# Loads at the start of a fused transformer kernel: parameter columns first, input rows in four parts, a shorter run of filler products, and the sum of the first norm later in the first weight unit

## The reference, cut to what matters

```
def rmsnorm(x, g):
    y = x * rsqrt(mean(x * x, axis=-1) + EPS)
    return y * g

h = rmsnorm(x, ab_norm)
z = h @ w_in                       # 1024 -> u, gate, q, k, v (512 each) and 8 forget logits
u, gate, q, k, v, f_logit = split(z)
y_a = rg_lru(causal_depthwise_conv(u, conv_w, conv_b), ...) * gelu(gate)
```

## Time and profile before

| | |
|---|---|
| median of three runs | 1609.82 us (1608.34 to 1611.64) |
| profiled execution, its own time | 1608.58 us |
| its span on the core | 1606.8 us |
| TensorE matmuls busy | 1447.0 us (90%) |
| VectorE busy | 765.9 us (48%) |
| ScalarE busy | 297.5 us (19%) |
| mean traffic | 247 GB/s |

### The profile page before, as it was taken

How to read it: one execution, slowest core, us unless ns; L and a number is a source line. 1 busy time by engine, 2 the same in 40 slices (tenths; PEclk the granted TensorE clock), 3 DMA queues, 4 the chain that set the end, 5 groups by cost and what they waited for, 6 DMA issues and landing times.

```text
span 1606.8 us, 23542 instructions
## 1 busy us (share of the span) xinstructions
PE 1447.0 (90%) x10020; PEld 1131.5 (70%) x10020; DVE 765.9 (48%) x1564; ACT 297.5 (19%) x745; POOL 29.2 (2%) x51
## 2 busy tenths in 40 slices
PE   9999999999999999999999999999987666667665
PEld 7779989998888799899988878778843212213121
DVE  6637617878676465188786877623220000000000
ACT  1332012220042410133100341332111001000000
POOL 0000000000001000000000030000000000000000
PEclk9999999999999999999999999999999878878787
DMA  9525415767444054158674104333899999999998
GB/s 394 226 79 209 158 53 223 291 240 282 169 157 159 1 210 158 53 223 324 262 284 164 53 1 132 102 133 153 366 424 427 429 428 429 428 427 428 428 431 332
DMA packets 47176, 396.51 MB, mean 247 GB/s; under 512 B 16352, under 2 KB 20192, under 8 KB 22624
## 3 DMA queue, kind: packets, MB, share of 16 engines
q1 hardware_dynamic: 45600, 393.51, 61.2%
q10 hardware_dynamic: 1472, 1.49, 0.3%
HBM read 392.36 MB, written 2.63 MB: 246 GB/s over the span
## 4 chain that ended last, share of the span: by engine, by line
PE 73%; DMA 22%; DVE 2%; SPq 1%; issue 0%; ACT 0%; DVEq 0%; ACTq 0%
PE pb L526 30%; DMA arena<-in_w_experts 16%; PE pb L1118 12%; PE pb L1082 11%; PE pb L626 7%; DMA ring<-in_w_experts 5%; PE pb L993 5%; PE pb L1026 3%; PE pb L1167 2%; PE pb L921 1%; PE pb L1193 1%; PE pb L697 1%; SPq L1729 1%; DMA ring<-in_w_dense 1%; DVE arena L3131 1%; DVE arena L3129 0%
## 5 line engine op out<-in xcount | busy, mean ns | idle before, releaser
L526 PE MATMUL pb<-hT,ring 128*128 128x256 f32 x768 | 175.4, 386 | 3.1 <-DMA ring<-in_w_dense 3.1
L526 PEld LDWEIGHTS pb<-hT,ring 128*128 128x128 f32 x768 | 145.9, 193 | 29.2 <-issue 5.8
L526 PE MATMUL pb<-ring,hT 128*32 128x512 f32 (+2 forms) x704 | 113.0, 686 | 46.9 <-DMA ring<-in_w_experts 45.7
L3303 DVE SCALAR_TENSOR_TENSOR side<-side,pb 128x256 f32<-128x256 f32 x16 | 6.7, 421 | 268.9 <-ACT side L1789 268.9
L626 PE MATMUL pb<-arena,ring 128*128 128x256 f32 x512 | 118.2, 382 | 0.0
L526 PEld LDWEIGHTS pb<-ring,hT 128*32 128x32 f32 (+1 forms) x704 | 32.8, 133 | 116.2 <-issue 63.2
L1789 ACT ACTIVATE arena<-pb 128x512 f32<-128x512 f32 (+4 forms) x124 | 54.2, 457 | 321.1 <-PE pb L526 120.2
L626 PEld LDWEIGHTS pb<-arena,ring 128*128 128x128 f32 x512 | 94.9, 190 | 14.6 <-issue 2.9
L1789 ACT ACTIVATE side<-pb 128x256 f32<-128x256 f32 (+2 forms) x58 | 23.1, 406 | 406.5 <-PE pb L526 389.8
L526 PE MATMUL pb<-arena,hT 128*32 128x512 f32 x248 | 40.7, 775 | 37.4 <-DMA arena<-in_w_experts 23.1
L526 PE MATMUL pb<-arena 128*64 128x128 f32 (+4 forms) x464 | 61.0, 331 | 0.8 <-ACT arena L1789 0.8
(11 more groups left out here) (476 smaller groups left out, 2501.0 us busy)
## 6 DMA issues: line engine op xcount, KB each, us to landing
ring<-in_w_dense SPq DMA_DIRECT2D x85, 2048.0 KB, 7.9
ring<-in_w_experts SPq DMA_DIRECT2D x56, 2048.0 KB, 44.6
arena<-in_w_experts SPq DMA_DIRECT2D x18, 2048.0 KB, 43.9
extra<-in_w_experts SPq DMA_DIRECT2D x10, 2048.0 KB, 44.4
arena<-in_w_experts SPq DMA_DIRECT2D x9, 1024.0 KB, 42.6
cons<-in_w_experts SPq DMA_DIRECT2D x9, 1024.0 KB, 44.9
ring<-in_w_dense SPq DMA_DIRECT2D x2, 1536.0 KB, 6.6
ring<-in_w_dense SPq DMA_DIRECT2D x4, 512.0 KB, 8.6
```

The lines of the kernel that those rows point to most:

```text
L526: return nc.tensor.matmul(o, l, r, start=st, stop=sp)
```

## The change

`cols` moves from ScalarE's queue to the front of SP's, with a semaphore of its own. `xT` is copied in four parts of two chunks (256 KB) with four semaphores: the first part ahead of unit 0, each other part behind one of the unit's first three quarters. VectorE and ScalarE wait for each part ahead of its two chunks. TensorE no longer waits for `cols` itself, the filler products are 14 instead of 20, and the norm's product stands after k = 5 instead of k = 2.

```
-        x_in, mem_in, out_sent = sem("x_loaded"), sem("mem_loaded"), sem("out_sent")
+        x_in, mem_in, out_sent = [sem(f"x_part{i}_loaded") for i in range(4)], sem("mem_loaded"), sem("out_sent")
@@ TensorE
-                    if k == 2:
+                    if k == 5:
                         norm_of_sum("ab")
             pe.wait_ge(filler_ready, 1)
-            for i in range(20):
+            for i in range(14):
                 nc.tensor.matmul(pb[:, 3, 0:P], epsm, epsm, start=True, stop=True)
-            pe.wait_ge(small_in, 32)
+            pe.wait_ge(small_in, 16)
             first_unit()
@@ SyncE
-            sp.dma_start(xT, a["xT"].rearrange("(c p) t -> p c t", p=P)).then_inc(x_in, 16)
+            def load_x(i):
+                rows_ = a["xT"].rearrange("(c p) t -> p c t", p=P)
+                sp.dma_start(xT[:, 2 * i:2 * i + 2, :], rows_[:, 2 * i:2 * i + 2, :]).then_inc(x_in[i], 16)
+            sp.dma_start(cols[:, :], a["cols"]).then_inc(cols_in, 16)
+            load_x(0)
@@ in the loop over the quarters of unit 0
                         sp.dma_start(t[:, at:at + UNIT][:, part], w[:, part]).then_inc(first_part[i] if i < 3 else loaded[slot_of[u]], 16)
+                        if i < 3:
+                            load_x(i + 1)
@@ ScalarE
-            act.dma_start(cols[:, :], a["cols"]).then_inc(small_in, 16)
-            act.wait_ge(x_in, 16)
-            squares(xT)
-            act.wait_ge(small_in, 32)
+            for c in range(DC):
+                if c % 2 == 0:
+                    act.wait_ge(x_in[c // 2], 16)
+                fn(sq[:, c, :], xT[:, c, :], ACT.Square).then_inc(norm_sq, 1)
+            act.wait_ge(small_in, 16)
+            act.wait_ge(cols_in, 16)
             root("ab")
@@ VectorE
-            dve.wait_ge(small_in, 32)
-            dve.wait_ge(x_in, 16)
+            dve.wait_ge(cols_in, 16)
             for c in range(DC):
+                if c % 2 == 0:
+                    dve.wait_ge(x_in[c // 2], 16)
                 V.tensor_scalar(raw_x[:, c, :], xT[:, c, :], col("ab_norm", c), None, ALU.mult).then_inc(raw_x_ready, 1)
             sum_pairs("ab")
```

More of the change, by code:

```diff
@@ L342, in program @@
         small_w_in, filler_ready = sem("small_weights_loaded"), sem("filler_rows")
-        small_in, late_in, lru_w_in = sem("small_loaded"), sem("constants_loaded"), sem("lru_w_loaded")
-        x_in, mem_in, out_sent = sem("x_loaded"), sem("mem_loaded"), sem("out_sent")
+        cols_in, small_in, late_in, lru_w_in = sem("columns_loaded"), sem("small_loaded"), sem("constants_loaded"), sem("lru_w_loaded")
+        x_in, mem_in, out_sent = [sem(f"x_part{i}_loaded") for i in range(4)], sem("mem_loaded"), sem("out_sent")
         hs_ready, raw_x_ready = sem("h_scaled"), sem("first_raw_rows")
```

## The result

The changed kernel takes 1615.07 us (median of 7 runs, 1613.18 to 1615.89), the kernel before, run beside it, 1610.55 us (7 runs, 1608.34 to 1611.92). The ratio is 1.003 with a 95% interval of 1.002 to 1.0039, that is 4.8 us slower by the ratio, between 3.2 and 6.3 (the two medians lie 4.5 apart). The forecast was 1610.1 with a range to 1612.8: the sign of the sum was right, its size far too small, and the range too short at its upper end.

The account below looks back on a forecast made before the run. TensorE, busy 90% of the span, was taken as the bound. Earlier start -2.65 and new wait +2.89 give +0.24 on 1608.58, so 1608.8; the median lies 1.24 above: 1610.1 us, range 1606.9 to 1612.8.

Parts of the forecast that it names:

- the sum: Shift of `ab_gate`, carried to the end: -2.65 us from the earlier start, +2.89 from the new wait, together +0.24.
- The new wait: TensorE ahead of `ab_gate` waits 2.89 us for VectorE's L2424 to free bank 0; bounded by 2.3 and 3.4.
- S - 6.06: Shift of `ab_gate`'s start, S + 20.85 against 26.91 before; +0.24 us with S = 6.30.
- S: Start of TensorE's first unit: 6.30 us, 8.95 before; bounds 6.1 and 6.8, or 7.2 with slow fillers.
- The working: Landing of unit 0's first quarter: 0.996 MB moved by about 5.40 us, plus 0.83 to landing, gives 6.23.
- The upper bound of 6.8: Limit on S if ScalarE's `small_w` (224 KB, 0.57 us) is moved entirely ahead of unit 0's first quarter.
- rival D: Unit 0's first quarter lands no earlier, at 8.2 us; S = 8.3, sum +2.2, 1612.1 us; chance 0.05.
- C: Pause ahead of `ab_gate` halves TensorE's clock, losing 1.7 to 3.4 us; +1.9 to +3.6, 1611.8 to 1613.5; chance 0.16.
- The covers: Slack before further waits: sum of squares 2.4 us, `hT` half a microsecond, later chunks over 4, recurrence 15.
- The aside: The norm's product, left behind k = 2, would stand at 11.7 us and wait nearly 3 us.
- a landing of the quarter at 5.0: Skill-page estimate for unit 0's first quarter: 0.73 + 2.0 + 0.996 MB / 436 GB/s; fillers would set S = 6.1.

Follow-up runs that it names:

- norm_k5: The kernel before with the norm's product after k = 5 instead of k = 2; 1.002 of before, 3.2 us slower.
- hold_rest: The changed kernel with bank 0 read first and SP issuing nothing behind the first quarter until x part 0 landed; 1613.25 and 1608.26 us, one run each.
- norm_k5_again: The same kernel as norm_k5, executed once more for a second profile; no time given, first scores at 89.80 us.
- small_late_only: The changed kernel with one edit, `small_w` issued only after x part 0 has landed; 1.0009 of before (0.9999 to 1.0019).
- all_k2: The changed kernel with the norm's product after k = 2 instead of k = 5; 1615.71 us, one run.
- parts_behind: The changed kernel with bank 0 read first and x parts 1 to 3 issued behind all four quarters of unit 0; 1613.23 us, one run.
- small_late: The changed kernel with bank 0 read first and `small_w` issued only after x part 0 has landed; 1608.60 us, one run.
- small_late_timed: The same program as small_late, executed again and timed; 0.9988 of before (0.9973 to 1.0003).

## Why the prediction was wrong, step by step

**The new wait: right.** "[A] new wait of 2.89 us, for VectorE's L2424" is 2.88 us for the same instruction. The formula "a difference of S - 6.06" holds: with the measured S = 7.72 it gives +1.66, measured +1.72; in norm_k5, S = 8.86, +2.80 and +2.85.

**S: the term that was mis-sized.** "I take S = 6.30" is 7.35 to 8.05 in three executions, 1.4 us too little in the profiled one. The working took the bytes ahead of the quarter at the pace at which the kernel before had moved its one large copy, and 0.83 us to landing. That takes for granted that nothing behind the quarter is moved before it is complete, and that the pace holds. Neither did. The traffic of the changed kernel from 4 to 7 us:

```profile
4.00:5.00 1.00, 1.00 (x6) 1.00 (x6) 0.00 (x0) 0.00 (x0) 0.00 (x0) 1.00 0.86 252
5.00:6.00 1.00, 1.00 (x7) 1.00 (x6) 0.61 (x2) 0.72 (x2) 0.00 (x0) 1.00 0.88 295
6.00:7.00 1.00, 0.81 (x7) 0.62 (x6) 0.00 (x0) 0.00 (x0) 0.00 (x0) 1.00 0.92 317
```

It is below the 403 GB/s of the earlier trace rows. By 7 us some 1.5 MB had been moved in all (a sum over the windows of one microsecond), 0.5 MB more than the 0.996 MB that the working counts, so `small_w` and copies behind the quarter have part of it. The quarter landed 6.0 us after its issue, at 7.65. The upper bound of 6.8 came from one extra copy only, `small_w`, and so was too low; rival D had the right direction (8.3) and got 0.05. What made the quarter late stays open: holding back what is behind it brought 6.7 and 6.4, but at the head of the queue, with everything behind it, it landed at 4.6. The dip in traffic is unexplained too; hold_rest has one as well (312 and 238 GB/s from 4 to 6).

**The clock: the rival that came.** C was priced right and weighed wrong. Its "1.7 to 3.4 us" measured 1.65 in each of the changed kernel's three profiles, the lower end. The sum put this term at nothing, and C was given 0.16 because 2.89 us was shorter than the only long pause shown. Of six pauses of 2.86 to 2.89 us ahead of `ab_gate`, five were followed by the half clock (the changed kernel three times, norm_k5_again, small_late_only) and one was not (norm_k5); those of 2.4 (all_k2) and 2.2 us (parts_behind) were followed by it as well. Pauses up to 1.59 us (norm_k5, ahead of the first unit) were followed by none. The Trainium skill's warning, TensorE: Matmul & The Clock Gate, section on HAM oscillation, was named in the forecast. Its direction is borne out, but the pauses here were shorter than those it warns of, and the measurement decides.

**The sum.** -1.23 from the start, +2.88 from the wait and +0.07 of spacing give the +1.72 measured at `ab_gate`; the clock 1.65; together +3.4, as measured at the scores and at 1019 us. The forecast's +0.24 lacks 1.4 of S and 1.65 of the clock. Against the measured 4.8 (3.2 to 6.3) that leaves 1.4 at the middle of the interval and nothing at its lower end.

**The covers: right.** The sum of squares was ready ahead of the norm's product, `ab_f` did not wait for `hT`, no later chunk of the unit waited, and the convolution and recurrence hid what they were said to hide: the shift at the gate is the shift at the scores wherever the clock holds. The aside that behind k = 2 the product "would wait nearly 3 us" measured 2.38. By the Trainium skill, DMA: Bandwidth & Descriptors, section Anatomy of one DMA, the forecast estimated a landing of the quarter at 5.0; it landed at 7.65, so a fixed cost plus the bytes in front was too little here. That section's figures are for copies issued by GpSimd, and these come from SP.

The one version whose interval lies below before reads the bank first, issues the first quarter first and `small_w` late: 0.9988 of before (0.9978 to 0.9998), 1.9 us.

## What to carry to other kernels

Moving a product later in TensorE's order moves everything that hangs on its result, on every engine; look for the PSUM bank that is freed at the end of that chain and for unrelated small work that stands ahead of the freeing instruction. A new pause of TensorE of two to three microseconds is to be priced with the half clock behind it as the likely case, here 1.7 us on top of 2.9. And when a copy must land early, don't take the bytes ahead of it at full pace for its landing: here that was 1.4 us short, and the same copy moved by 1.2 us between two executions of one program.

## What the runs showed of the hardware

The clock fell behind pauses of 2.2 to 2.9 us in seven of eight cases, for 3.0 to 3.4 us each time, and identical programs differed in it (norm_k5). It also fell with no pause at all, behind 32 instructions of 32 columns, in six of eighteen profiles. The landing of the same quarter moved the first product from 6.58 to 7.80 between two executions of one program (small_late and small_late_timed). An instruction of a filler product costs 0.22 us at first and 0.12 later, while the windows print a granted clock of 1.00 throughout; the change of pace comes earlier or later, so that the end of the 28 filler instructions lay between 5.9 and 7.4 us.
